# The row minimum as the exponential's bias: query weights and mixer logits with the opposite sign

## The reference

```
ql = rms_norm(pq, q_norm);  kl = rms_norm(pk, k_norm);  rope on both
s  = einsum('btgrd,blgd->bgrtl', q, k) * (64 ** -0.5)
p  = softmax(s);            y = p @ v
```

## Time and profile before

| what | value |
|---|---|
| time, median of 3 runs | 1556.15 us (1555.81 to 1556.73) |
| the profiled execution | 1554.53 us, of it span 1552.6 us |
| busy: TensorE, VectorE, ScalarE | 1387.1, 680.1, 528.5 us |
| mean granted TensorE clock | 0.928 of full speed |
| trunk attention, layer 0 | about 183 to 394 us from the span's start |
| trunk attention, layer 1 | about 812 to 920 us |
| mixer attention | about 1179 to 1226 us |
| experts | 1257 us to the end |

### The profile page before, as it was taken

One profiled execution on the slowest core, in us unless ns is written; L12 is line 12 of the kernel. 1 busy time (PEld: TensorE's weight loads), 2 busy tenths in 40 slices (PEclk: granted clock), 3 DMA queues, 4 the chain that ended last, 5 costly groups with the idle time before them and its releaser, 6 DMA issues. The chain is left out here.

```text
span 1552.6 us, 19336 instructions
## 1 busy us (share of the span) xinstructions
PE 1387.1 (89%) x7886; PEld 1050.7 (68%) x7886; DVE 680.1 (44%) x1321; ACT 528.5 (34%) x854; POOL 43.5 (3%) x36
## 2 busy tenths in 40 slices
PE   6999896778999999998989779999698868999996
PEld 3887574555678888877867559998485446666663
DVE  3222536774132433558445854556516333222122
ACT  2225332343442322415544447444226221111112
POOL 0000000210000000002000110000000000000000
PEclk9999998798699999998999988999798878999998
DMA  9422121114320424224422003455132644999990
GB/s 386 169 102 82 54 81 55 55 55 169 130 81 27 163 89 156 109 81 144 140 105 81 28 1 108 164 191 190 43 136 81 267 180 184 410 405 409 410 401 32
DMA packets 34222, 238.96 MB, mean 154 GB/s; under 512 B 4304, under 2 KB 4432, under 8 KB 6224
## 3 DMA queue, kind: packets, MB, share of 16 engines
q1 hardware_dynamic: 34128, 237.66, 40.1%
HBM read 236.59 MB, written 1.05 MB: 153 GB/s over the span
## 5 line engine op out<-in xcount | busy, mean ns | idle before, releaser
L226 DVE TENSOR_TENSOR pieces_lo<-weight_ring,pieces_hi 128x1024 fp32r<-128x1024 f32 x154 | 186.9, 1223 | 311.2 <-ACT pieces_hi L218 311.2
L244 PE MATMUL proj<-h_hi,pieces_hi 128*128 128x512 f32 (+1 forms) x816 | 288.7, 354 | 7.3 <-DVE pieces_lo L226 3.7
L246 PE MATMUL proj<-h_hi,pieces_lo 128*128 128x512 f32 (+1 forms) x816 | 284.7, 349 | 0.0
L245 PE MATMUL proj<-h_lo,pieces_hi 128*128 128x512 f32 (+1 forms) x816 | 283.2, 347 | 0.0
L218 ACT ACTIVATE pieces_hi<-weight_ring 128x1024 fp32r<-128x1024 f32 x158 | 165.4, 1053 | 237.7 <-PE score L246 149.9
L244 PEld LDWEIGHTS proj<-h_hi,pieces_hi 128*128 128x128 f32 x816 | 156.3, 191 | 36.2 <-issue 14.7
L245 PEld LDWEIGHTS proj<-h_lo,pieces_hi 128*128 128x128 f32 x816 | 156.3, 191 | 22.8 <-issue 1.7
L246 PEld LDWEIGHTS proj<-h_hi,pieces_lo 128*128 128x128 f32 x816 | 155.9, 191 | 20.0
L1854 PE MATMUL turn<-expert_parts,e_gathered 128*64 128x256 f32 x768 | 85.3, 379 | 0.0
L1854 PEld LDWEIGHTS turn<-expert_parts,e_gathered 128*64 128x64 f32 x768 | 55.1, 137 | 32.3 <-issue 6.3
L733 PE MATMUL turn<-l_diag,l_probs 128*128 128x128 f32 x320 | 46.9, 301 | 32.7 <-DVE l_diag L1151 15.7
(11 more groups left out here) (410 smaller groups left out, 2121.1 us busy)
## 6 DMA issues: line engine op xcount, KB each, us to landing
weight_ring<-in_stream SPq DMA_DIRECT2D x110, 1024.0 KB, 5.1
expert_parts<-in_experts SPq DMA_DIRECT2D x70, 1024.0 KB, 10.8
weight_ring<-in_experts SPq DMA_DIRECT2D x26, 1024.0 KB, 10.9
l_rows<-in_rows SPq DMA_DIRECT2D x2, 768.0 KB, 15.6
l_y_attn<-in_ada_first SPq DMA_DIRECT2D x1, 1024.0 KB, 5.4
l_y_gla<-in_ada_first SPq DMA_DIRECT2D x1, 1024.0 KB, 7.5
l_y_sgu<-in_ada_first SPq DMA_DIRECT2D x1, 1024.0 KB, 8.4
l_q<-in_ada_first SPq DMA_DIRECT2D x1, 1024.0 KB, 10.2
```

The costliest lines, as they stand in the source:

```text
L226: eng.tensor_tensor(self.part(self.lo_ring[:, n % NPIECE, :], kind), self.raw(slot, c, kind), self.part(self.hi_ring[:, n % NPIECE, :], ki ...
L244: pe.matmul(out, sh, mh, start=start, stop=False)
L245: pe.matmul(out, sh, ml, start=False, stop=False)
L246: return pe.matmul(out, sl, mh, start=False, stop=stop)
```

## The change

The column of query norm weights is multiplied by -1/8 once a layer, so that the trunk's scores come out scaled and with the opposite sign. Their row minimum is then the bias that the exponential needs, and the exponential runs with scale -1. In the mixer, decay, mask and scores are put together with the opposite sign; the row minimum is the bias there too.

```diff
+        q_norm = sb("q_norm", [P, 1])
...
                         act.activation(PR[:, i % 2, u, 0:n], PS.tile(J("score", i, u))[:, 0:n], ACT.Exp,
-                                       bias=small[:, i % 2, 2 + u:3 + u], scale=0.125,
+                                       bias=small[:, i % 2, u:u + 1], scale=-1.0,
...
                 if (kind, i) == first_use:
                     dve.wait_ge(*sig.small_in.at(small_in))
+                    link(dve.tensor_scalar(q_norm[:], par[:, A_QN:A_QN + 1], -0.125, None, ALU.mult))
...
-                    w = A_KN if i == 0 else A_QN
+                    w = par[:, A_KN:A_KN + 1] if i == 0 else q_norm[:]
...
-                    dve.scalar_tensor_tensor(x, x, par[:, w:w + 1], rstd, ALU.mult, ALU.mult).then_inc(*sig.normed.one())
+                    dve.scalar_tensor_tensor(x, x, w, rstd, ALU.mult, ALU.mult).then_inc(*sig.normed.one())
...
                         dve.wait_ge(*PS.ready(J("score", i, u)))
-                        link(dve.reduce_max(small[:, i % 2, u:u + 1], PS.tile(J("score", i, u))[:, 0:n], AX.X))
-                        dve.tensor_scalar(small[:, i % 2, 2 + u:3 + u], small[:, i % 2, u:u + 1], -0.125, None,
-                                          ALU.mult).then_inc(*sig.neg_max.one())
+                        dve.tensor_reduce(small[:, i % 2, u:u + 1], PS.tile(J("score", i, u))[:, 0:n], AX.X, ALU.min)\
+                            .then_inc(*sig.neg_max.one())
...
-                        act.activation(PR[:, i % 2, u, 0:n], LG[:, u, 0:n], ACT.Exp, bias=small[:, i % 2, 2 + u:3 + u],
+                        act.activation(PR[:, i % 2, u, 0:n], LG[:, u, 0:n], ACT.Exp, bias=small[:, i % 2, u:u + 1], scale=-1.0,
...
-                        link(dve.tensor_scalar(lg, CB[:, h, 0:n], CT[:, t, h:h + 1], -1.0, ALU.subtract, ALU.mult))
+                        link(dve.tensor_scalar(lg, CB[:, h, 0:n], CT[:, t, h:h + 1], None, ALU.subtract))
...
-                        dve.scalar_tensor_tensor(lg, PS.tile(J("score", i, u))[:, 0:n], 0.125, lg, ALU.mult, ALU.add)\
+                        dve.scalar_tensor_tensor(lg, PS.tile(J("score", i, u))[:, 0:n], -0.125, lg, ALU.mult, ALU.add)\
...
-                        link(dve.reduce_max(small[:, i % 2, u:u + 1], lg, AX.X))
-                        dve.tensor_scalar(small[:, i % 2, 2 + u:3 + u], small[:, i % 2, u:u + 1], -1.0, None,
-                                          ALU.mult).then_inc(*sig.neg_max.one())
+                        dve.tensor_reduce(small[:, i % 2, u:u + 1], lg, AX.X, ALU.min).then_inc(*sig.neg_max.one())
...
-    c[:, M_CAUSAL:M_CAUSAL + P] = np.where(r[None, :] <= r[:, None], 0, -1e30)
+    c[:, M_CAUSAL:M_CAUSAL + P] = np.where(r[None, :] <= r[:, None], 0, 1e30)
```

## The result

The changed kernel takes 1541.94 us in the median of 10 runs (1535.85 to 1544.04), the kernel before 1555.98 beside it (10 runs): ratio 0.991, 95% interval 0.9895 to 0.993. The profiled executions are 1554.53 and 1543.51 us.

What follows compares the result with a forecast made beforehand. TensorE's waits in attention and mixer, on VectorE's diagonal matrix and ScalarE's copies, were where gains could pay. Layer 0 3.7, layer 1 2.1 and mixer 1.8 summed to 7.6 us: 1548.6 us, range 1544.5 to 1553.0.

Steps and rivals of the forecast that it cites:

- the collisions: Layer 0, two VectorE products slowed to 1.49 us beside GpSimd's: bounds 0 and 2.4 us gained, 0 put in the sum.
- Both chains arrive together: Layer 1's repeating units: VectorE and ScalarE end equally late, so ScalarE's 0.19 us a period counts, 5 units, 0.95 us.
- the second one gains no more: Trunk, second exponential of a pair: queued on ScalarE behind the first and its accumulator read, it gains no more than 0.19 us.
- the clause for the upper bound: Layer 1: if VectorE's 0.37 us counted in all units, 0.9 us more than the 2.1 us summed.
- Layer 0's 3.7 us: Trunk, 16 units: eight at 0.37 us by VectorE, four at 0.19 by ScalarE, four at nothing; sum 3.7 us.
- ScalarE, 0.19: Layer 0, units 1, 2, 4, 15: the chain goes by ScalarE's queue, 0.19 us each, 0.76 us.
- The mixer's 1.8 us: Mixer, 8 units: 0.38 us before each of TensorE's four waits on the copy, 0.64 at the first; sum 1.8 us.
- The clock rival: Dense products after layer 0: TensorE stays at 1.2 GHz longer, kernel slower; with 35 us more it ends at 1566; 4%.
- More than the sum: Rival: VectorE's 0.37 us in all 24 trunk units, 8.9 instead of 5.8, and both collisions go, 2.4; 1543 us; 10%.
- Given away at once: Rival: another TensorE wait takes over, or slack was taken for a chain; less than 3.1 us left, 1554.5 us; 10%.
- The prices: Trunk: reductions 0.60 us apart, pair 1.21, exponential 0.72 after its reduction; 62 fewer VectorE instructions; minimum equal to maximum, immediates nothing.
- The rival that the wait costs nothing: Trunk and mixer: 0.72 us is the reduction's own time, VectorE gains only 0.14 a unit; 4.3 us, 1551.9 us; 10%.

Runs made afterwards that it cites:

- linked multiply: Changed kernel plus, behind each trunk reduction, a multiply that waits for it and that nobody waits for: 1548.2 us, ratio 0.996; in layer 0 only: 1543.47 us.
- free multiply: Changed kernel plus, behind each trunk reduction, a one-column multiply of another column that waits for nothing: 1545.63 us.
- the two meetings alone: Changed kernel plus a multiply waiting for each reduction, awaited by nobody, only in units 8 and 13 of layer 0: 1546.52 us, ratio to before 0.993.
- the mixer alone: Kernel before with only the mixer's part of the change, trunk as before: 1551.29 us, ratio 0.9965.
- the trunk alone: Changed kernel with the mixer of the kernel before, so only the trunk's part of the change: 1544.34 us, ratio 0.992.
- one linked: Changed kernel plus a multiply that waits for the reduction and that nobody waits for, behind the second reduction of each trunk pair only: 1549.34 us.

## Why the prediction was wrong

**The step that failed first** is the sentence on the collisions, "so I put 0 in the sum and leave the rest to the range". Both dissolved, and the experiment that brings back only these two costs 4.6 us by the medians and 3.5 in its profile from the first reciprocal of layer 0 to its last product (187.9 us against 184.0 to 184.4 in three of the changed kernel's four). 0.6 and 1.2 us are the steps themselves; their sum, 1.8, is inside the bounds of 0 to 2.4. The other 1.56 (10.50 less 8.94) was in no bound: it is TensorE's clock in the turn behind unit 13, 3.47 us against 2.03. The step from 13 to 14 was 1.4 to 1.6 us longer in six of the ten profiles with a meeting in unit 13 (two of the four of before, both kernels with the linked multiply in all of layer 0, the free multiply, the two meetings alone), and in none of the eight without one. So in this kernel the meeting often costs the clock too.

**"Both chains arrive together", so that 0.19 us counts in a period of layer 1**, was a misread row. I took the accumulator read's duration as the time until ScalarE is free; the next instruction starts 0.09 us after the read's start. VectorE decided alone and gave its 0.37. Also wrong was "the second one gains no more": the second exponential was released by its own multiply (873.75 in a period that starts at 872.07, 1.68 later, against 865.24 and 863.84, 1.40), so ScalarE's part came forward by 0.28 and did not hold the gain back. The seven steps of layer 1 gave 2.4 us, by the clause for the upper bound, not the 1.7 that stood for them in the sum.

**Layer 0's 3.7 us** came out well as a sum, not in its parts. Without units 8 and 13 the steps give some 3.5 to 3.8 us. But the four units put at "ScalarE, 0.19" owe nothing to ScalarE (the linked multiply takes all of it away), and the plain steps give 0.38 to 0.41.

**The mixer's 1.8 us** became 1.3 in the window that the prediction meant, up to the start of the output projection (45.9 before and 44.6 after on the mean of four). The terms in front of each of TensorE's waits were right (the wait at the second copy 1.04 before and 0.85 after, the last one 3.34 and 2.96), but the gates behind them run longer at the lower clock, by 0.20, 0.43 and 0.63 us. Part of that comes back in front of them: four matmuls of `turn` ahead of the third gate take 0.77 us after and 1.09 before. The prediction read the clock of this window, 0.79, and priced it in no term.

**The clock rival** expected a loss and priced only that; the prediction gave the clock no term of its own in the sum. It came out with the opposite sign. Here is where the 11.5 us between the means of the four profiles lie:

| stretch | gained, us | of it the change's own steps |
|---|---|---|
| layer 0, units 0 to 15 | 7.8 | about 5.5 (the two meetings 1.8) |
| layer 1, units 16 to 23 | 3.4 | 2.4 |
| mixer up to the output projection | 1.3 | 1.3, net of the gates |
| output projection to the first expert | 0.8 | 0, same instructions |
| everything else | -1.7 | 0; 0.9 of it at the start |

So the change's own steps make about 9 and a better clock about 4; 1.7 are lost elsewhere. Behind the mixer these are 0.8. In the trunk three places show the lower clock in TensorE's rows: behind unit 13 (0.7), in front of unit 17 (1.0: long in all four profiles of before, in one of four after), and from 8 to 10 (1.0). At the last of these, before the change, either two groups of matmuls late in the second step take 3.64 and 1.98 us (2.75 and 1.90 after), or a turn early in the first takes 3.48 (2.05 after). The remaining 0.6 of layer 0 lie in steps that swing in both kernels and were not traced.

Whether the change itself makes the better clock likelier is told by the other profiles. From 8 to 10 it looks so: 22.7 to 22.8 us in six of the seven profiles in which VectorE's queue in layer 0 is as long as before, and at most 21.2 in the eleven others. For the step in front of unit 17 it is not shown: it was short with the mixer alone, whose trunk is that of before, and long with the trunk alone.

The medians differ by 14.0 (first comparison). The prediction took 3.1 us as what the measurement can tell from no change, from three runs within 0.9 us of each other; the 85 runs spread far wider. What the medians have beyond 11.5 stays open: four profiles show a shorter stretch at the lower clock behind layer 0, but why an execution falls into one group or the other was not found.

**Luck and the nearest rival.** "More than the sum", 1543 us at 10%, came closest to the 1541.94, and its account of the meetings and of layer 1 is the one that the runs bear out. VectorE's 0.37 did not come in all 24 units, though; the clock filled the gap, and that is luck. In the rival "Given away at once" the mean wait of 1.6 us is a little more than four gains of 0.37, which make 1.48; no term hangs on it.

**What held.** The prices: 62 instructions, 0.72 to the exponential, 0.60 between reductions, 1.20 to 1.21 for the pair; no price for the minimum, the new multiplies (146 ns each) or the altered immediates; the expert stage, from the first expert's matmuls on, 252.5 to 252.7 us before and 252.6 to 252.8 after, once 253.7. The rival that the wait costs nothing is refuted by the free multiply. The Trainium skill, page VectorE: DVE Perf Modes, section The DRAIN you can't avoid, would have a semaphore cost nothing extra; here the multiply starts 0.60 us after the reduction without a wait and 0.72 with one. The Trainium skill's page SBUF — State Buffer, by which whichever of GpSimd and a VectorE instruction with two SBUF inputs starts first keeps the shared ports for its whole instruction, agrees with all the meetings: 0.05 us decided between 0.69 and 1.49 us for VectorE. Seven more such pairs stand in layer 0, in which VectorE is first by 0.04 to 0.12 us before the change already and GpSimd's product takes 1.70 to 1.78. Only the length is not quite the sum: 1.27 and 0.69 would make 1.96, and VectorE ends 1.81 to 1.83 us after GpSimd's start.

## What to carry to other kernels

A one-column instruction with a wait behind it costs a busy in-order queue about 0.19 us, more than half of it the wait, and it pays each time where that queue carries the chain: fold it into a factor that is applied earlier anyway, or do two columns at once. Before you call two chains equally late, look at when the instruction behind an accumulator read starts, not at the read's duration. Where a transfer of work moves an engine by tenths of a microsecond across another's start, price both outcomes and what TensorE's clock does behind them; a sum with 0 there is a choice, and here it was the wrong one.

## What was not expected of the hardware

- When VectorE's product meets GpSimd's in layer 0, the order hangs on 0.05 us. First in line, VectorE takes 0.69 us and GpSimd 1.78 in place of 1.27. Coming 0.12, 0.19 or 0.38 us later (free multiply, one linked, two linked), VectorE takes 1.76, 1.68 and 1.50: it ends at about the same moment, however early it arrives.
- Exponentials of 512 elements with an accumulator read stand 0.68 us apart when queued (864.56 to 865.24), though exponential and read last 0.69 and 0.19 us.
- Executions of one kernel fall into groups some 10 to 17 us apart. In four profiles one sees where: behind layer 0, for instance 394 to 430 us, at a granted clock of 0.76 and 1.00 in place of 0.50, 7.1 us shorter in that profile and some 4 to 5 in the other three (the step from 15 to 16).
